# Squared-ReLU MLP in a diffusion backbone: seven products on sums of weight and token parts for 20 of 32 column tiles

## The chip, the cores and the metric

One Trainium2 chip, one core. The metric is the device time of one execution in microseconds (us), the median of three runs. The program is written for the engines directly: each engine (TensorE as PE, VectorE as DVE, ScalarE as ACT, GpSimd as POOL, and SP, which issues most DMAs) runs its own list of instructions in order, and the lists meet only at semaphores.

## The reference

Four layers, each a token mixer (Fourier, gated convolution, RWKV-7, latent attention) followed by a dense MLP, on 512 latent and 128 context tokens (640 columns, T) with D = 1024 features. All is float32. Cut to the MLP:

```
h = rmsnorm(x, g4[2]) * (1 + m[4]) + m[3]          # m: six modulation vectors of the layer
o = square(relu(h @ mlp_w1[i])) @ mlp_w2[i]        # (640 x 1024) @ (1024 x 4096), then @ (4096 x 1024)
x = x + m[5] * rmsnorm(o, g4[3])
```

The modulation vectors are `silu(c) @ mod_w[i] + mod_b[i]`, a matrix of 1024 x 6144 per layer.

## The kernel before

Features lie on the 128 partitions, tokens along the free axis. A weight tile ("slab") is 128 output features by all 1024 inputs, 512 KB. To keep float32 precision each operand is split into a high part (rounded to the type `fp32r`, which PE takes) and a low part (the rest). A product is three matmuls for each block of 128 inputs: high by high, high by low, low by high. SP loads a slab into `wr`, ACT copies it rounded into `ws[..., 0, :]` (`high_part`, line 1757), POOL subtracts (`low_part`, line 771), and PE reads both. `wr` and `ws` have two buffers each, so the loop load, copy, subtract, load goes over two tiles.

The tokens are taken whole (a full tile: 8 blocks x 3 products x 2 halves of 320 tokens = 48 matmuls of 128x320) or by halves (a half tile: 24 matmuls). The MLP of a layer is 32 column tiles of W1 and 32 of W2, the latter in four blocks over the hidden features:

- `in_halves`: 8 tiles of W1 and 8 of W2, first all for the first half of the tokens, then all for the second. The first half overlaps the norm of the rest. PE lines 903 (high) and 913 (low).
- 5 blocks of 8 full tiles: W1, W2, W1, W2, W1 (`unit`, PE lines 882 and 887). For W1, ACT makes the relu (line 2432) and the rounded square (2434); DVE makes the exact square (3340) and its low part (3344) in `hidden_unit`. For W2, DVE adds the tile into `acc` (`out_block`).
- `out_halves`: the last 8 tiles of W2 by halves, with the next norm between them.

Beside the full tiles DVE works on the modulation vectors of the next layer: `mods_beside` takes one or two of 48 tiles per full tile (56 in layer 0, where 8 are left over). A tile (`mod_tile`, line 2711) is two multiply-and-accumulate operations of 128x1024 with `silu` held in PSUM (`silu_near`, copied at line 3368). Its 512 KB come through three or four buffers (`mr`, `mx`) by SP. The lists of ACT, DVE and SP are loops (`Fori`) in this part.

The lists are hand-ordered; each engine takes its instructions strictly in the order of the text, a wait included.

## Time and profile before

| | |
|---|---|
| median of 3 runs | 3523.78 us (3521.26 to 3525.21) |
| profiled execution | 3521.14 us, span 3519.1 us |
| PE busy | 3241.9 us, 92% of the span, 29266 matmuls |
| DVE busy | 1811.0 us, 51% |
| POOL busy | 1564.5 us, 44% |
| ACT busy | 1282.7 us, 36% |
| TensorE clock, mean granted | 0.973 |
| DMA | 465.68 MB, mean 132 GB/s |

Read it so: the shares of busy time are means over very different stages. In the rwkv stage PE waits; in the MLPs it hardly does. Matmuls overlap in the records (each is listed with some 309 ns, though they start 147 ns apart), so for their cost the distance from one start to the next counts.

### The profile page before, as it was taken

How to read it: one execution, taken by the hardware profiler on the slowest of the kernel's cores; microseconds unless marked ns; L12 is line 12 of the kernel's file. 1: busy time of each engine (PE TensorE's matmuls, PEld its weight loads, DVE VectorE, ACT ScalarE, POOL GpSimd, SP SyncE). 2: the span in 40 equal slices, each digit the busy share in tenths (PEclk: the TensorE clock that was granted, in tenths of full speed). 3: DMA queues.
4: the chain of work that ended last, by engine and by line, in shares of the span. 5: the costliest groups of instructions: out<-in, count | busy, mean ns of one | idle time of the engine just before them, and what ended most of it. 6: DMA issues, size and time to landing. Idle time of an engine off the chain costs nothing.

```text
span 3519.1 us, 74842 instructions
## 1 busy us (share of the span) xinstructions
PE 3241.9 (92%) x29266; PEld 3007.5 (85%) x29266; DVE 1811.0 (51%) x3092; ACT 1282.7 (36%) x2148; POOL 1564.5 (44%) x1043
## 2 busy tenths in 40 slices
PE   5899999999999998898688889999998989999998
PEld 2789999899899997796577777999997856899997
DVE  8643765564526555859834444447545643521113
ACT  5343223422532224546423334432234333532223
POOL 0455334554553334535577744643344301563334
PEclk9899999999999999999899999999999999999999
DMA  7544554333345443436734433445443301342223
GB/s 285 161 124 148 195 202 141 121 114 100 113 141 196 158 143 109 124 120 221 238 102 119 119 77 120 126 150 197 148 145 97 99 3 37 114 144 73 77 72 122
DMA packets 209306, 465.68 MB, mean 132 GB/s; under 512 B 89056, under 2 KB 98848, under 8 KB 208544
## 3 DMA queue, kind: packets, MB, share of 16 engines
q1 hardware_dynamic: 179904, 442.50, 39.0%
q10 hardware_dynamic: 29152, 19.65, 1.8%
q8 instruction: 182, 2.98, 0.3%
q14 instruction: 68, 0.56, 0.0%
HBM read 419.71 MB, written 41.06 MB: 131 GB/s over the span
## 4 chain that ended last, share of the span: by engine, by line
issue 65%; POOL 17%; POOLq 8%; PE 5%; DVE 3%; DVEq 1%; ACT 0%; DMA 0%; ACTq 0%; SPq 0%
POOL ws L771 17%; POOLq L811 4%; POOLq L808 3%; PE banks L903 1%; PE banks L882 1%; PE banks L913 1%; PE banks L887 1%; POOLq L779 1%; PE banks L1178 0%; DVE bt L2992 0%; POOLq L817 0%; DVEq L2982 0%; DVEq L3022 0%; DVE ar L3011 0%; DVE bt L3014 0%
## 5 line engine op out<-in xcount | busy, mean ns | idle before, releaser
L771 POOL TENSOR_TENSOR ws<-wr,ws 128x1024 fp32r<-128x1024 f32 x509 | 1239.6, 2436 | 1814.5 <-ACT ws L1757 1813.1
L1757 ACT ACTIVATE ws<-wr 128x1024 fp32r<-128x1024 f32 x509 | 537.8, 1057 | 1029.2 <-PE banks L887 442.0
L882 PE MATMUL banks<-hs,ws 128*128 128x320 f32 x3712 | 564.9, 309 | 0.4 <-DVE acc L2833 0.3
L882 PEld LDWEIGHTS banks<-hs,ws 128*128 128x128 f32 x3712 | 549.0, 188 | 1.6 <-DVE hs L2935 0.7
L903 PE MATMUL banks<-hs,ws 128*128 128x320 f32 (+2 forms) x2624 | 446.2, 320 | 43.8 <-DVE hs L2570 14.2
L903 PEld LDWEIGHTS banks<-hs,ws 128*128 128x128 f32 x2624 | 404.4, 194 | 71.5 <-issue 29.8
L903 PE MATMUL banks<-fs,ws 128*128 128x320 f32 x2304 | 374.3, 312 | 12.8 <-DVE fs L3326 6.4
L2711 DVE SCALAR_TENSOR_TENSOR mjunk<-mr,banks 128x1024 f32<-128x1024 f32 x286 | 337.9, 1219 | 72.2 <-DMA mr<-in_m_slabs 49.2
L903 PEld LDWEIGHTS banks<-fs,ws 128*128 128x128 f32 x2304 | 343.9, 188 | 31.5 <-issue 12.5
L882 PE MATMUL banks<-fs,ws 128*128 128x320 f32 x2048 | 310.8, 309 | 0.0
L882 PEld LDWEIGHTS banks<-fs,ws 128*128 128x128 f32 x2048 | 303.0, 188 | 0.0
L887 PE MATMUL banks<-hs,ws 128*128 128x320 f32 x1856 | 291.0, 309 | 0.0
L887 PEld LDWEIGHTS banks<-hs,ws 128*128 128x128 f32 x1856 | 277.0, 188 | 0.0
L913 PE MATMUL banks<-hs,ws 128*128 128x320 f32 (+2 forms) x1312 | 232.5, 319 | 2.5 <-POOL ws L771 2.5
L2432 ACT ACTIVATE relu<-banks 128x640 f32<-128x640 f32 x92 | 64.9, 705 | 427.1 <-PE banks L887 427.1
L913 PEld LDWEIGHTS banks<-hs,ws 128*128 128x128 f32 x1312 | 206.0, 194 | 13.6 <-issue 8.0
L913 PE MATMUL banks<-fs,ws 128*128 128x320 f32 x1152 | 195.7, 311 | 0.0
L913 PEld LDWEIGHTS banks<-fs,ws 128*128 128x128 f32 x1152 | 174.4, 188 | 3.9 <-POOL ws L771 2.2
L810 POOL TENSOR_TENSOR inv_x<-inv_x,inv_t 80x31 f32<-80x31 f32 (+15 forms) x248 | 151.3, 610 | 36.1 <-issue 1.3
L887 PE MATMUL banks<-fs,ws 128*128 128x320 f32 x1024 | 160.6, 309 | 0.0
L806 POOL TENSOR_TENSOR inv_t<-inv_a,inv_x 80x31 f32<-80x31 f32 (+15 forms) x248 | 143.4, 578 | 36.1 <-issue 1.7
L887 PEld LDWEIGHTS banks<-fs,ws 128*128 128x128 f32 x1024 | 152.8, 188 | 0.0
(332 smaller groups left out, 3960.1 us busy)
## 6 DMA issues: line engine op xcount, KB each, us to landing
wr<-in_w_slabs SPq DMA_DIRECT2D x509, 512.0 KB, 3.6
mr<-in_m_slabs SPq DMA_DIRECT2D x167, 512.0 KB, 5.1
ar_d<-ar SPq DMA_DIRECT2D x16, 640.0 KB, 4.3
bk_d<-bt SPq DMA_DIRECT2D x16, 640.0 KB, 6.1
bk<-bk_d SPq DMA_DIRECT2D x16, 640.0 KB, 5.5
ar<-ar_d SPq DMA_DIRECT2D x32, 320.0 KB, 5.4
mx<-in_m_slabs SPq DMA_DIRECT2D x16, 512.0 KB, 6.6
rkv_d<-relu ACTq DMA_DIRECT2D x16, 320.0 KB, 3.7
```

Of the source, the lines that this page charges most:

```text
L771: pool.tensor_tensor(ws[s % 2][:, 1, :], wr[:, s % 2, :], ws[s % 2][:, 0, :].bitcast(F32), ALU.subtract).then_inc(lo_ready, 1)
L806: pool.tensor_tensor(tj, blocks_in[:, j + 1:32, j:j + 1].to_broadcast(shape), x[:, j:j + 1, 0:j + 1].to_broadcast(shape), ALU.mult)
L808: pool.drain()
L810: pool.tensor_tensor(rows, rows, tj, ALU.add)
L811: pool.drain()
L882: pe.matmul(pu[:, t % 2, h, 0:HT], ws[s % 2][:, 0, k * P:(k + 1) * P], src[:, k, part, h * HT:(h + 1) * HT], start=(k + part == 0), stop=F ...
L887: mm = pe.matmul(pu[:, t % 2, h, 0:HT], ws[s % 2][:, 1, k * P:(k + 1) * P], src[:, k, 0, h * HT:(h + 1) * HT], start=False, stop=(k == KD ...
L903: pe.matmul(pu[:, t % 2, h, 0:q - p], ws[s % 2][:, 0, k * P:(k + 1) * P], src[:, k, c, p:q], start=(k + c == 0), stop=False)
L913: mm = pe.matmul(pu[:, t % 2, h, 0:q - p], ws[s % 2][:, 1, k * P:(k + 1) * P], src[:, k, 0, p:q], start=False, stop=(k == KD - 1))
L1757: act.activation(ws[s % 2][:, 0, :], wr[:, s % 2, :], ACT.Copy).then_inc(hi_ready, 1)
L2432: act.activation(halves(relu[:, j, :]), pu[:, t % 2, :, 0:HT], ACT.Relu).then_inc(relu_ready, 1)
L2711: op = dve.scalar_tensor_tensor(mjunk[:, g, :], at, 0.5, vector[:, g, :], ALU.mult, ALU.mult, accum_out=modt[:, col, g:g + 1].rearrange("p ...
```

## The change

W1's tiles 12 to 31 of each layer are taken in ten pairs. A pair is seen as a matrix of 2 x 2: two column tiles by two halves of the 1024 inputs (A11 to A22, each 128 x 512). The tokens are seen as 2 x 2 too: two halves of the inputs by two halves of the tokens (B11 to B22). The eight products of the plain rule become seven, on four sums of weight parts and four sums of token parts (`t1`, `t2`, `t34`), and the results are added up from PSUM. A product is 4 blocks x 3 = 12 matmuls of 128x320.

- POOL (`weight_pairs`) makes the weight sums in float32: four additions of 128x512 per pair, then one low part per product. ACT makes the high parts and copies three partial results out of PSUM per pair. The operands of PE are in a ring of four places of 128x512 (`wq`, over the old `ws`), so a place is written again only after its last product.
- The token sums are made during the second half of `in_halves`: `combine_copy`, `combine_high` on ACT and `combine_part` on DVE, for four rows in four steps each. `t34` has no room of its own and lies over `x`, so ACT's queue stores `x` (2.6 MB) to `x_d` when the second half starts and reads it back after the last pair; the next use of `x` waits for it.
- W2's tiles 8 to 23 are cut into quarters of 128x512 (`U_ENTRY`), each for four hidden blocks. The first eight pairs have four quarters each: eight products more, whose results DVE adds into `acc` (`take_u`). So a pair has 15 products, the last two pairs have 7.
- Before the pairs stand 4 full tiles of W1 (`regular`).
- The raw pair comes as one load of 1 MB into `wp`, a single new buffer, for the last pair into `wr`. The silu vectors are read back from memory in each of the first three layers (1 MB, through `wp`) in place of lying in SBUF.
- Modulation tiles: two after each of the four full tiles, then five per pair (six in layer 0); `mx` is gone, three buffers are left.
- All lists of this part are written out, no loops.

The core of the diff. PE's order for one pair, where `product(n, step, e, bank, tokens, fresh)` is one product with entry e of the ring:

```diff
+                for n in range(PAIRS):
+                    dense = n >= PAIRS_U
...
+                    if n == 0:
+                        pe.wait_ge(tile_read, t_out - 1)
+                    elif n <= PAIRS_U:
+                        pe.wait_ge(u_taken, u0 - 3)
+                    else:
+                        pe.wait_ge(f_ready, f1 - 2)
+                    product(n, 1, 0, xb, b11, True)
...
+                    product(n, 2, 1, yb_, first, True)
+                    pe.wait_ge(part_copied, copied + 1)
+                    product(n, 3, 2, xb, second, False)
...
+                    product(n, 4, 3, zb, b21, True)
+                    pe.wait_ge(part_copied, copied + 3)
+                    product(n, 5, 4, xb, third, False)
...
+                    product(n, 6, 5, wb, h0, True)
+                    pe.wait_ge(sum_made, summed + 1)
+                    product(n, 7, 6, yb_, b22, False)
+                    product(n, 8, 7, xb, fourth, False)
+                    pe.wait_ge(u_taken, u0 + 1)
+                    product(n, 9, 5, wb, h1, True)
+                    pe.wait_ge(f_ready, f1 + 2)
+                    product(n, 10, 8, zb, h0, True)
+                    pe.wait_ge(f_ready, f1 + 3)
+                    product(n, 11, 8, yb_, h1, True)
+                    pe.wait_ge(f_ready, f1 + 4)
+                    product(n, 12, 9, xb, h0, True)
+                    pe.wait_ge(u_taken, u0 + 2)
+                    product(n, 13, 9, wb, h1, True)
+                    pe.wait_ge(u_taken, u0 + 3)
+                    product(n, 14, 10, zb, h0, True)
+                    pe.wait_ge(u_taken, u0 + 6)
+                    product(n, 15, 10, wb, h1, True)
```

In `product`, PE waits for `e_high` before the 8 matmuls on the high part and for `e_low` before the 4 on the low part. DVE's list:

```diff
+                for i in range(KH):
+                    regular(i)
+                    mods(2)
+                for n in range(PAIRS_U):
+                    mods(2)
+                    dve.drain()
+                    corner_sum(n)
+                    first_sum(n)
+                    dve.drain()
+                    square(n, 0)
+                    square(n, 1)
+                    dve.drain()
+                    square_low(n, 0)
+                    square_low(n, 1)
+                    take_u(n, 0)
+                    second_sum(n)
...
+                    square(n, 2)
+                    square(n, 3)
...
+                    square_low(n, 2)
+                    square_low(n, 3)
+                    take_u(n, 1)
+                    mods(1)
+                    take_u(n, 2)
+                    take_u(n, 3)
+                    mods(1)
+                    take_u(n, 4)
+                    take_u(n, 5)
+                    mods(1)
+                    take_u(n, 6)
+                    take_u(n, 7)
+                    mods(mods_in_pair(l) - 5)
```

`corner_sum` waits for product 5 and adds bank xb and `c_sum`, which lies in SBUF; `square(n, 0)` and `square_low(n, 0)` read only SBUF. POOL's list, and SP's loads of the raw pairs:

```diff
+                sums(0)
+                more_sums(0)
+                for e in range(3):
+                    low(0, e)
+                last_sum(0)
+                low(0, 3)
+                for n in range(PAIRS):
+                    if n < PAIRS_U:
+                        for e in range(4, 11):
+                            low(n, e)
+                        sums(n + 1)
+                        more_sums(n + 1)
+                    elif n < PAIRS - 1:
+                        low(n, 4)
+                        sums(n + 1)
+                        low(n, 5)
+                        low(n, 6)
+                        pool.drain()
+                        more_sums(n + 1)
...
+                    for e in range(3):
+                        low(n + 1, e)
+                    last_sum(n + 1)
+                    low(n + 1, 3)
...
+                def load_pair(m):
+
+                    if m == 0:
+                        sp.wait_ge(t_made, 9 * li + 9)
+                    if m:
+                        sp.wait_ge(e_low, from_ahead + ENTRIES * li + entry_at(m - 1, 10 if m == PAIRS - 2 else 7) + 1
+                                   if m < PAIRS - 1 else from_ahead + ENTRIES * li + entry_at(PAIRS_U - 1, 10) + 1)
+                    to = wr if m == PAIRS - 1 else wp
+                    sp.dma_start(to[:, :, :], a["w_slabs"][d + 2 * m:d + 2 * m + 2].rearrange("s p n -> p s n")
+                                 ).then_inc(p_landed[m == PAIRS - 1], 16)
...
+                load_pair(PAIRS - 1)
+                sp.wait_ge(e_low, from_ahead + ENTRIES * (li + 1))
```

ACT's list for the last two pairs ends, and for the last pair holds the copy of the first slab behind them (`high_part`):

```diff
+                    squared(n, 0)
+                    squared(n, 1)
+                    if n < PAIRS - 1:
+                        highs(n + 1, 1)
+                    else:
+                        act.wait_ge(product_done, product_at(li, n, 5))
+                        high_part(slab[0], None)
+                    positive(n, 2)
+                    act.drain()
+                    squared(n, 2)
...
+                    positive(n, 3)
+                    act.drain()
+                    squared(n, 3)
...
+                act.dma_start(x[:, :, :].rearrange("p k n -> p (k n)"), x_d).then_inc(x_moved, 16)
```

## Rows read from the trace of the kernel before

**Rows 1.** The page's first part, PE: busy time, share of the span, instructions.
```profile
PE 3241.9 (92%) x29266; PEld 3007.5 (85%) x29266; DVE 1811.0 (51%) x3092; ACT 1282.7 (36%) x2148; POOL 1564.5 (44%) x1043
```

**Rows 2.** Windows: stretch, length, busy time of each engine, granted clock, DMA share, GB/s.
```profile
305.00:587.00 282.00, 282.00 (x1925) 282.00 (x1924) 186.16 (x289) 73.23 (x86) 97.74 (x41) 1.00 0.51 179
136.00:140.00 4.00, 4.00 (x24) 3.62 (x17) 0.05 (x1) 1.51 (x4) 2.39 (x1) 0.65 0.51 141
15.00:25.00 10.00, 0.00 (x0) 0.00 (x0) 7.78 (x13) 3.83 (x6) 0.00 (x0) 1.00 1.03 404
```

**Rows 3.** Timeline of PE, full and half tiles: start, length, line, operation, count.
```profile
305.37 4.86 PE L882 MATMUL banks<-hs,ws 128*128 128x320 f32 x32
312.41 4.86 PE L882 MATMUL banks<-hs,ws 128*128 128x320 f32 x32
...
268.92 2.51 PE L903 MATMUL banks<-hs,ws 128*128 128x320 f32 x16
272.44 2.51 PE L903 MATMUL banks<-hs,ws 128*128 128x320 f32 x16
```

**Rows 4.** Groups by line, PE: count, busy, mean ns, idle before, releaser.
```profile
L882 PE MATMUL banks<-hs,ws 128*128 128x320 f32 x3712 | 564.9, 309 | 0.4 <-DVE acc L2833 0.3
```

**Rows 5.** Groups by line and form, DVE.
```profile
L2711 DVE SCALAR_TENSOR_TENSOR mjunk<-mr,banks 128x1024 f32<-128x1024 f32 x286 | 337.9, 1219 | 72.2 <-DMA mr<-in_m_slabs 49.2 <-issue 22.1
...
L2627 DVE TENSOR_TENSOR acc<-banks,acc 128x320 f32<-128x320 f32 x64 | 31.4, 490 | 129.5 <-PE banks L913 119.5 <-PE banks L972 6.1 <-PE banks L948 3.6
```

**Rows 6.** Timeline of DVE, two modulation tiles back to back, their first halves.
```profile
582.70 1.22 DVE L2711 SCALAR_TENSOR_TENSOR mjunk<-mr,banks 128x1024 f32<-128x1024 f32 x1
...
585.16 1.22 DVE L2711 SCALAR_TENSOR_TENSOR mjunk<-mr,banks 128x1024 f32<-128x1024 f32 x1
```

**Rows 7.** Groups by line and form, ACT.
```profile
L1757 ACT ACTIVATE ws<-wr 128x1024 fp32r<-128x1024 f32 x509 | 537.8, 1057 | 1029.2 <-PE banks L887 442.0 <-DMA wr<-in_w_slabs 362.7 <-PE banks L913 180.1
...
L2289 ACT ACTIVATE tr<-banks 128x512 f32<-128x512 f32 x80 | 44.6, 602 | 61.5 <-PE banks L1417 61.5
...
L2006 ACT ACTIVATE reluh<-banks 128x320 f32<-128x320 f32 x64 | 26.8, 418 | 0.0
```

**Rows 8.** Groups by line and form, POOL.
```profile
L771 POOL TENSOR_TENSOR ws<-wr,ws 128x1024 fp32r<-128x1024 f32 x509 | 1239.6, 2436 | 1814.5 <-ACT ws L1757 1813.1 <-issue 0.2
...
L806 POOL TENSOR_TENSOR inv_t<-inv_a,inv_x 80x255 f32<-80x255 f32 x16 | 11.0, 690 | 2.3
```

**Rows 9.** DMA issues: transfer, queue, count, KB each, median us to landing.
```profile
wr<-in_w_slabs SPq DMA_DIRECT2D x509, 512.0 KB, 3.6
...
silu<-silu_d SPq DMA_DIRECT2D x1, 1024.0 KB, 6.8
```

**Rows 10.** Instructions of DVE's line 2524, both inputs in SBUF: shortest, median, longest ns.
```profile
L2524 DVE TENSOR_TENSOR rstd<-root,ident x30: 491/493/1830, 146.5 to 3505.1; 128x320 f32<-128x320 f32 x30
```

**Rows 11.** Timeline of DVE at the first full tile of W1.
```profile
313.46 0.83 DVE L3340 SCALAR_TENSOR_TENSOR ta<-banks,relu 128x640 f32<-128x640 f32 x1 [5.01 <-ACT relu L2432]
...
315.76 1.22 DVE L2711 SCALAR_TENSOR_TENSOR mjunk<-mr,banks 128x1024 f32<-128x1024 f32 x1 [0.31 <-DMA mr<-in_m_slabs]
```

**Rows 12.** Timeline of PE behind two waits (in brackets: idle time and its releaser).
```profile
135.70 0.74 PE L932 MATMUL banks<-sqa,ones 128*32 128x320 f32 x8 [2.53 <-DVE mjunk L2711]
136.38 4.00 PE L903 MATMUL banks<-hs,ws 128*128 128x320 f32 x16
...
622.49 0.35 PE L940 MATMUL banks<-rstd,ones 128*32 128x80 f32 x8 [1.73 <-ACT rstd L1795]
```

**Rows 13.** Timeline of ACT and PE where the second half of the tokens begins.
```profile
251.42 1.06 ACT L1757 ACTIVATE ws<-wr 128x1024 fp32r<-128x1024 f32 x1 [2.40 <-DMA wr<-in_w_slabs]
...
254.04 2.58 PE L903 MATMUL banks<-hs,ws 128*128 128x320 f32 x16 [1.05 <-DVE fs L3326]
```

**Rows 14.** Timeline of ACT and PE in the last block of W2.
```profile
596.21 1.06 ACT L1757 ACTIVATE ws<-wr 128x1024 fp32r<-128x1024 f32 x1 [4.03 <-DMA wr<-in_w_slabs]
...
597.53 2.51 PE L903 MATMUL banks<-fs,ws 128*128 128x320 f32 x16
```

More of the change, by code:

```diff
@@ L450, in build @@
         order = []
+        middles = []
         first_slab = 0
@@ L2052, in in_halves @@
                     take(j, 1)
-                for j in range(mid - 1):
-                    ahead()
+                    if hidden:
+                        combine_part(j, li)
+                for j in range(mid):
+                    if j < mid - 1:
+                        ahead()
+                    combine_part(n + j, li)
                 x_tiles[0] += 2 * KD
@@ new lines, in mlp @@
+            def mlp(li):
+                in_halves(FB, 4, True, li)
+                for i in range(KH):
+                    t = tile[0]
+                    if i < KH - 1:
+                        ahead()
+                    else:
+                        slab[0] += 1
+                        tile[0] += 1
+                        for e in range(2):
+                            entry_high(li, 0, e)
+                    act.wait_ge(tile_done, t + 1)
+                    act.wait_ge(tile_read, t - 1)
+                    act.activation(halves(relu[:, i % 2, :]), pu[:, t % 2, :, 0:HT], ACT.Relu).then_inc(relu_ready, 1)
+                    act.drain()
+                    act.activation(fs[:, i, 0, :], relu[:, i % 2, :], ACT.Square).then_inc(fhalf_ready, 1)
+                weight_pairs(li)
@@ L3401, in mlp @@
-                tile[0] += 5 * FB
-                hidden[0] += 3 * FB + 1
-                relus[0] += 3 * FB + 1
+                    dve.wait_ge(c_landed, xc_in + 16 * (l + 1))
+                    dve.tensor_copy(silu_near[:, :, :], wp[:, :, :])
+                dve.drain()
+                dve.sem_inc(t_made, 1)
+                t_out, mod_next = tile[0] + KH, [-M_LEFT if l == 0 else 0]
+                assert t_out == middle_tile[l]
+                for i in range(KH):
+                    regular(i)
+                    mods(2)
```

610 lines of the change are left out of this document (441 added, 169 removed).

## Prediction

> **What bounds the kernel now.** I read the page first: TensorE (PE) is busy for 92% of the span and no other engine for more than 51% [rows 1]. That share is a mean over stages, so I asked the stage windows for the part that the change replaces, the 40 full tiles of an MLP (W1 tiles and W2 tiles of 640 tokens). There PE is busy 282.00 of 282.00 us at full granted clock [rows 2]. In the timeline one full tile follows the next after 7.04 us, and one half tile (320 tokens) the next after 3.52 us [rows 3]. A full tile is 48 matmuls, so one matmul of 128x320 costs 146.7 ns. The groups say that this holds everywhere: 3712 matmuls of line 882 have 0.4 us of idle time before them [rows 4]. So here a matmul less is worth its full 146.7 ns, and every wait that the new order brings to PE costs its full length. Nothing hides either.
>
> **The saving.** Two column tiles cost 96 matmuls now. As seven products of 12 matmuls they cost 84. Ten pairs in each of four layers: 12 x 10 x 4 = 480 matmuls fewer, 480 x 0.1467 = **70.4 us**. W2's tiles keep their count: eight products per pair are two tiles' worth. A product is 12 x 0.1467 = 1.76 us, a pair with W2 quarters (15 products) 26.4 us, one without (the last two) 12.3 us. The rest is a ledger of waits.
>
> **Prices.** DVE: 0.49 us for an operation of 128x320 with one input in PSUM, 1.22 us for each half of a modulation tile [rows 5]; two such tiles back to back start 2.46 us apart [rows 6]. ACT: 1.06 us for a copy of 128x1024, 0.60 for 128x512, 0.42 for 128x320 [rows 7]. POOL: 2.44 us for 128x1024; no group has 128x512, so from 80x255 at 0.69 us the line between the two gives 1.27 us (half of the large one, 1.22, is the lower bound) [rows 8]. A load of 512 KB lands after 3.6 us; the fastest stretch moved 404 GB/s, so 0.5 MB more ahead of it costs 1.3 us; 1 MB lands between 4.9 us by that sum and the 6.8 us of the one row that has it [rows 2, 9].
>
> **Steady pairs, by laying the four lists side by side** (us from the start of a pair). POOL: 15 operations x 1.27 = 19 of 26.4. ACT: 11 copies, 3 part copies, 8 for relu and square, 12 us. DVE: 19 operations x 0.49, five or six modulation tiles x 2.46 and drains, 22 to 25 us. So none is the bound by its sum; the order decides. Product 5 ends at 8.8; corner sum 9.5; ACT relus 10.2; squares and low parts of the first two quarters to 13.1; the first W2 take 13.6 (product 9 needs it at 14.1). The second sum, two squares and lows end at 17.2, the take behind them 17.7; modulation tile 20.2, two takes 21.3, tile 23.8, takes four and five 24.9. Product 15 needs that fifth take at 24.6. So PE waits about **0.35 us a pair** where there are modulation tiles (layers 0 to 2), none in layer 3. Seven pairs (the first is counted below): 2.5 us a layer. This includes 0.8 us for one DVE square whose inputs both lie in SBUF while POOL works: the trace has 30 operations of such a kind (128x320) with a median of 493 ns and a longest of 1830 [rows 10]. Without it the take is at 24.1, in time, and the term is 0; with the longest at both such operations of a pair it is up to 8.
>
> The Trainium skill, "SBUF — State Buffer", section "SBUF: two separate sides", says that a VectorE operation with two SBUF inputs and a GpSimd operation that reads SBUF exclude each other for a whole instruction. The trace agrees as far as [rows 10] go; by that rule the sum has the 2.5 us, without it 0.
>
> **First pair, layers 0 to 2.** Before, one or two modulation tiles went beside each full tile; now two follow each of four W1 tiles and two more stand before the first corner sum. From the trace, DVE takes its first tile 8.1 us after PE began it [rows 11, 3], a W1 tile's two operations cost 2.1 (2.30 to the tile behind them, less the most of its 0.31 wait for a load). From 8.1: 4 x 2.1 + 10 x 2.46 = 33.0, so 41.1, and the corner sum ends at 41.6. PE wants it before product 7, at 4 x 7.04 + 6 x 1.76 = 38.7. Wait 2.9 us. After a wait of 2.53 us the trace shows 16 matmuls in 4.00 us, where others take 2.51, with the granted clock at 0.65 of full, between its levels 2.4 and 1.2 GHz; after 1.73 us the matmuls kept their pace [rows 2, 3, 12]. So add 1.5: **4.5 us** a layer (2.9 to 7), x 3 = 13.5. Queued behind those tiles on SP is the slab of the fourth W1 tile: its load waits for a modulation buffer, about 15.4, and it comes just in time; no extra.
>
> **Second half of the first 16 tiles.** Sixteen combination steps go onto ACT and DVE, and x (2.6 MB) is stored from ACT's queue just as this half starts. Sums fit: ACT gets 4 x 0.42 more in every other tile of 3.5 us. But ACT takes a tile's relu only after its next slab copy, which waits for the slab's DMA, and PE waits for that take already (1.05 us) [rows 13]. So a load made 1.3 us longer by the store goes to PE in full; DVE's four extra operations (2 us) before a take add some 1.2 over the half. **2.5 us** x 4 = 10; nothing as lower bound, 6 with two loads hit and the clock lowered. The load of 1 MB for the modulation vectors now stands among these slabs (layers 0 to 2): 2.6 us of transfer, less about 2 of slack: 0.7 x 3 = 2.
>
> **Into the last two pairs.** SP loads pair 8 only after POOL's last low part of pair 7, at 19.5 on pair 7's time. Landed at 24.5 to 26.3, then three sums and a low part, 5.1: 29.6 to 31.4. PE needs it at 26.4 + 1.2. From there POOL has 15 operations (19.0 us) up to the first low part of pair 9, while PE's matmuls up to it last 13.5. Pair 9 can so end at 24.5 + 19.0 + 0.6 + 6 x 1.76 = 54.7 (26.3: 56.5) where the products alone end at 51.0. **4.5 us** x 4 = 18, bounds 3 (POOL at 1.22) and 6.5.
>
> **Into the second matrix's last tiles.** Now the loads run ahead and PE goes on at once; ACT's copy ends just before its tile, 596.21 + 1.06 against 597.53 [rows 14]. After the change the raw pair 9 lies in both slab buffers, so the first slab can be loaded only after POOL's very last low part, 2.0 before pair 9 ends. 3.6 for the load and 1.06 for the copy: PE idle 2.7. ACT does its last two squares only after that copy, and PE waits for them after 14 matmuls: 0.5. x is read back (6.5 us of transfer) beside the next slab: 1.3 more, partly under a lowered clock (up to 1.5). **4.5 us** x 4 = 18, bounds 2.5 and 9. x itself is wanted 28 us later: hidden.
>
> **Sum.** Waits 7.5 + 13.5 + 10 + 2 + 18 + 18 = 69. Against the saving: -1.4. The profiled execution took 3521.1 us for a span of 3519.1; the median of the three runs is 3523.8, 2.7 above it. 3521.1 - 1.4 + 2.7 = **3522 us**. All lower bounds: 0 + 8.7 + 0 + 0 + 12 + 10 = 31, 3484. All upper ones: 24 + 21 + 24 + 6 + 26 + 36 = 137, 3590.
>
> **Rivals.** (1) The same waits, near their lower bounds, because one wait gives the other engines the time that the next would have cost: total about 35, so 3488. For it: the terms are laid out one after the other, and PE's wait into pair 8 lets DMA and ACT run ahead. Against: the two waits for loads have fixed lengths that no engine shortens. (2) Slower: the fifth take decides. If both operations on the corner sum wait for POOL, or a modulation tile waits for its load, it comes 1.5 us late in every pair; 8 x 3 x 1.5 = 36 in place of 7.5: 3550. It decides from 24.6 us on; my own time for it is 24.9, so the margin is thin. (3) The change doesn't bring its saving: PE waits on two semaphores per 12 matmuls in place of two per 24 or 48. If each product lost 0.1 us, 536 products would give 54: 3576. Against: half tiles with as many matmuls per wait as now 24 and 8 run at 146.7 ns [rows 3].
>
> **Chances.** The ledger as summed, 3507 to 3540: 0.46. Rival 1: 0.33. Rival 2: 0.17. Rival 3: 0.04. A measurement tells 0.2% (7 us) from no change. Faster: rival 1 and a fifth of the first, 0.42; same: half of the first, 0.23; slower: the rest, 0.35. The range 3488 to 3556 leaves out the ends of both sides; as both signs hold much chance, the likeliest case's own is 3507 to 3540.
>
> **What would show it.** Right: products 1.76 us apart; PE idle near 3 us before product 7 of the first pair with DVE as releaser, 2 to 4 us in product 1 of pair 8 behind POOL, about 3 us before the first tile of the last W2 block behind ACT and a slab load. Wrong: a wait in every pair much over 0.35 us (rival 2), these three below 1 us each (rival 1), or a product longer than 1.76 us without a wait (rival 3).

## Result and the profile after

The changed kernel takes 3555.9 us (median of 4 runs, 3554.1 to 3566.8), the kernel before 3523.5 beside it: ratio 1.0099, 95% interval 1.0078 to 1.0120: 32 us slower by the medians, 35 by the ratio, which the table of experiments uses. Forecast were 3522 us, 3507 to 3540 for the likeliest case, and most of the chance on faster or the same; the result lies above that, at the end of the wider range (3556). The profiled execution took 3556.7 us for a span of 3554.9, 35.8 more than before.

The page of the changed kernel: the first part, then groups by line (the answers to [rows 1, 4, 8]) and DMA issues (to [rows 9]).

```profile
PE 3209.8 (90%) x28786; PEld 2971.0 (84%) x28786; DVE 2062.0 (58%) x3756; ACT 1481.6 (42%) x2812; POOL 1944.1 (55%) x1467
...
L1059 PE MATMUL banks<-hs,ws 128*128 128x320 f32 (+2 forms) x2624 | 452.7, 324 | 62.3 <-DVE fs L3729 24.6
...
L1059 PE MATMUL banks<-fs,ws 128*128 128x320 f32 x2304 | 386.6, 319 | 43.9 <-ACT ws L2014 28.1
...
L1897 PE MATMUL banks<-fs,wq 128*128 128x320 f32 x2048 | 342.0, 309 | 0.0
...
L903 POOL TENSOR_TENSOR wq<-wp,wq 128x512 fp32r<-128x512 f32 x144 | 185.3, 1298 | 16.7 <-issue 11.3
...
L1897 PE MATMUL banks<-hs,wq 128*128 128x320 f32 x960 | 163.1, 313 | 11.6 <-DVE c_sum L3776 9.7
...
wr<-in_w_slabs SPq DMA_DIRECT2D x429, 512.0 KB, 3.7
...
wp<-in_w_slabs SPq DMA_DIRECT2D x36, 1024.0 KB, 5.1
x_d<-x ACTq DMA_DIRECT2D x4, 2560.0 KB, 9.0
x<-x_d ACTq DMA_DIRECT2D x4, 2560.0 KB, 10.0
```

The reader is to see three things. PE has 480 matmuls less, and is busy only 32.1 us less. The products (L1897) have hardly an idle moment: 0.0 in the largest group, 11.6 us in the one whose waits are those of the first pairs. Most of the new idle time sits in L1059, the half tiles on either side of the new part: 62.3 and 43.9 us, where the same two groups of the kernel before (L903) had 43.8 and 12.8. And x's transfers last 9 and 10 us.

To place it, I took from PE's timeline the start of each stage in each layer, and the distances between them (us; layers 0, 1, 2, 3). "Last block" runs to the next stage's first matmul, in layer 3 to the end of the span. The forecast's ledger stands beside them as the sum over four layers.

| stage | before | after | more, 4 layers | forecast |
|---|---|---|---|---|
| second half of the first 16 tiles | 59.8 60.9 59.8 59.9 | 66.1 67.8 68.4 67.0 | +29.0 | +12 |
| 4 full tiles of W1 (28.2) | | 29.3 29.5 28.4 28.2 | +2.8 | 0 |
| first pair (26.4) | | 34.3 30.8 30.8 26.7 | +17.0 | +13.5 |
| pairs 1 to 7 (184.8) | | 184.8 in each | -0.1 | +7.5 |
| last two pairs (24.6) | | 30.5 30.3 30.1 30.4 | +22.8 | +18 |
| gap ahead of the last block | | 2.8 2.9 3.0 3.0 | +11.8 | with the last block |
| last block of W2 | 67.7 76.3 65.4 79.2 | 72.6 83.6 72.4 85.5 | +25.5 | +18 with the gap |
| all waits | | | +108.8 | +69 |
| matmuls saved | | | -70.4 | -70.4 |
| the rest of the kernel | | | -2.4 | 0 |

In brackets stand the lengths at 146.7 ns a matmul. Sum +36.0, the spans say +35.8.

Now the two large rows. Timeline of the changed kernel, ACT and PE, where the second half begins in layer 0 (answers to [rows 13]):

```profile
247.79 0.33 ACTq L2333 DMA_DIRECT2D x_d<-x  x1
...
252.22 1.06 ACT L2014 ACTIVATE ws<-wr 128x1024 fp32r<-128x1024 f32 x1 [3.37 <-DMA wr<-in_w_slabs]
...
254.85 3.43 PE L1059 MATMUL banks<-hs,ws 128*128 128x320 f32 x16 [2.02 <-DVE fs L3729]
...
259.56 1.06 ACT L2014 ACTIVATE ws<-wr 128x1024 fp32r<-128x1024 f32 x1 [4.00 <-DMA wr<-in_w_slabs]
...
262.19 3.86 PE L1059 MATMUL banks<-hs,ws 128*128 128x320 f32 x16 [2.06 <-DVE fs L3729]
```

Read it from below: PE waits for `fs`, the low part of DVE's square, which waits for ACT's relu, which stands behind a slab copy, which waited 4.00 us for its DMA. Before, PE waited 1.05 us at the first place [rows 13] and 0.17 at the second. And after each wait 16 matmuls take 3.4 to 3.9 us in place of 2.6.

The last block in layer 0 (answers to [rows 14]), and under it the DMA queues in the 10 us from x's read-back on; q10 is ACT's queue, q1 is SP's (packets, MB, share of the 16 engines' time; then issue, KB each, median us to landing):

```profile
592.06 1.06 ACT L2014 ACTIVATE ws<-wr 128x1024 fp32r<-128x1024 f32 x1 [2.75 <-DMA wr<-in_w_slabs]
...
593.17 3.81 PE L1059 MATMUL banks<-fs,ws 128*128 128x320 f32 x16 [2.66 <-ACT ws L2014]
...
594.42 0.33 ACTq L2845 DMA_DIRECT2D x<-x_d  x1
...
595.77 3.10 SPq L530 DMA_DIRECT2D wr<-in_w_slabs  x2
...
605.10 1.06 ACT L2014 ACTIVATE ws<-wr 128x1024 fp32r<-128x1024 f32 x1 [9.18 <-DMA wr<-in_w_slabs]
...
606.20 4.63 PE L1059 MATMUL banks<-fs,ws 128*128 128x320 f32 x16 [4.20 <-ACT ws L2014]
```

```profile
q10 hardware_dynamic: 144, 2.62, 68.5%
q1 hardware_dynamic: 221, 0.85, 20.6%
...
x<-x_d ACTq DMA_DIRECT2D x1, 2560.0 KB, 10.2
wr<-in_w_slabs SPq DMA_DIRECT2D x2, 512.0 KB, 8.5
```

The first slab was issued at 595.8, 1.3 us behind x's transfer, and was there at 605.1, 9.3 us later and 0.5 us after x had landed; the second took 7.7 us (8.5 is the median of the two). A slab takes 3.7 us elsewhere. PE stood 4.20 us for it.

The trace has each packet's start, and the delay has two parts. Packets first: x goes in 144 for 2.62 MB, a slab in 144 for 0.52 MB; 16 of each are 4 bytes long, the other 128 are 20,480 bytes (x) and 4,096 bytes (slab). The queues in the first 3.4 us after the slab was issued (595.8 to 599.2), and in the 5.3 us after that (599.2 to 604.5):

```profile
q10 hardware_dynamic: 53, 1.09, 79.9%
```

```profile
q10 hardware_dynamic: 79, 1.29, 56.7%
q1 hardware_dynamic: 230, 0.88, 40.5%
```

In the first window SP's queue has no packet at all: the slab's first one comes 3.45 us after its issue, where a slab that meets no x transfer has it after 0.96 us (median of 217 in this kernel). In the second window the slab shares the engines with packets five times as long, and needs 5.9 us from its first packet to landing, where it needs 2.7 alone.

Windows of the two stages, the kernel before and then the changed one (stretch, length, busy time and instructions of each engine, granted clock, DMA share, GB/s):

```profile
245.00:305.00 60.00, 57.71 (x388) 56.55 (x387) 11.87 (x24) 23.54 (x33) 39.88 (x17) 1.00 0.48 148
...
587.00:655.00 68.00, 63.48 (x448) 58.51 (x448) 25.44 (x54) 31.18 (x52) 38.51 (x16) 1.00 0.42 125
```

```profile
245.00:311.00 66.00, 60.52 (x385) 59.32 (x384) 32.15 (x68) 34.05 (x64) 39.29 (x17) 0.95 0.54 188
...
593.00:666.00 73.00, 67.39 (x446) 62.31 (x447) 24.41 (x52) 31.10 (x53) 40.68 (x17) 0.93 0.45 153
```

In the second half PE is idle 5.5 us (66.00 less 60.52) where it was 2.3, and busy 2.8 us longer for the same matmuls, at a granted clock of 0.95 in place of 1.00: after the waits it ran for a time at 1.2 GHz, not 2.4. In the last block it is idle 1.1 us more and busy 3.9 us more. So in the second half the clock costs about as much as the added waits, in the last block more.

The first pair of layer 0, DVE and PE:

```profile
348.56 1.30 DVE L3144 TENSOR_TENSOR modt<-modt,modb 128x16 f32<-128x16 f32 x1
349.93 1.19 DVE L3150 SCALAR_TENSOR_TENSOR coef<-modt,ng 128x16 f32<-128x16 f32 x1
...
356.24 0.49 DVE L3776 TENSOR_TENSOR c_sum<-banks,c_sum 128x320 f32<-128x320 f32 x1 [0.16 <-issue]
...
356.78 2.50 PE L1897 MATMUL banks<-hs,wq 128*128 128x320 f32 x8 [5.04 <-DVE c_sum L3776]
```

PE waits for the corner sum as forecast, but 5.0 us in place of 2.9: the modulation coefficients (L3144, L3150; 348.56 to 351.24, 2.7 us) fall between the tiles in this layer.

A steady pair, pair 2 of layer 0, which starts at 401.50 (DVE):

```profile
411.58 1.33 DVE L3803 SCALAR_TENSOR_TENSOR c_sum<-c_sum,reluh 128x320 f32<-128x320 f32 x1 [0.19 <-ACT reluh L2787]
...
413.40 0.49 DVE L3812 SCALAR_TENSOR_TENSOR fs<-c_sum,fs 128x320 fp32r<-128x320 f32 x1
413.81 0.48 DVE L3815 TENSOR_TENSOR fs<-banks,fs 128x320 fp32r<-128x320 f32 x1
...
423.98 1.09 DVE L3825 TENSOR_TENSOR acc<-banks,acc 128x320 f32<-128x320 f32 x2
```

The square with both inputs in SBUF takes 1.33 us, as the ledger's 0.8 us more had it: of the kernel's 40 such squares 31 begin while POOL works, and 30 of these take 1.33 to 1.59 us; the other ten take 0.49. Even so takes four and five (the last line) are done at 425.07, 23.6 us after the pair's start, where 24.9 was forecast and product 15 wants them at 24.6. For DVE operations listed with 0.49 us follow one another after 0.4 us (413.40 to 413.81), and the forecast had priced them at 0.49.

### The profile page after: what moved, and what is told of

Read it like the earlier page. It is cut to its first block, busy times and chain, and to the rows that moved or that the text cites. A ratio compares the mean times of both kernels' runs of the same rounds, so it can differ in the third digit from the quotient of the medians.

```text
span 3554.9 us, 73409 instructions
## 1 busy us (share of the span) xinstructions
PE 3209.8 (90%) x28786; PEld 2971.0 (84%) x28786; DVE 2062.0 (58%) x3756; ACT 1481.6 (42%) x2812; POOL 1944.1 (55%) x1467
## 4 chain that ended last, share of the span: by engine, by line
issue 38%; PE 32%; POOL 12%; POOLq 10%; DVE 4%; DMA 1%; DVEq 1%; ACT 1%; ACTq 0%; SPq 0%
PE banks L1897 15%; POOL ws L844 10%; PE banks L1901 7%; POOLq L959 3%; PE banks L1059 3%; POOLq L956 3%; PE banks L1038 3%; PE banks L1069 2%; POOL wq L903 2%; PE banks L1043 1%; POOLq L870 1%; DMA wr<-in_w_slabs 1%; DVE mjunk L3127 1%; DVE mr L3127 1%; PE banks L1334 0%
## 5 line engine op out<-in xcount | busy, mean ns | idle before, releaser
L844 POOL TENSOR_TENSOR ws<-wr,ws 128x1024 fp32r<-128x1024 f32 x365 | 892.1, 2445 | 1199.9 <-ACT ws L2014 1199.3
L1059 PE MATMUL banks<-hs,ws 128*128 128x320 f32 (+2 forms) x2624 | 452.7, 324 | 62.3 <-DVE fs L3729 24.6
L1059 PEld LDWEIGHTS banks<-hs,ws 128*128 128x128 f32 x2624 | 411.0, 197 | 90.5 <-issue 49.3
L1059 PE MATMUL banks<-fs,ws 128*128 128x320 f32 x2304 | 386.6, 319 | 43.9 <-ACT ws L2014 28.1
L1059 PEld LDWEIGHTS banks<-fs,ws 128*128 128x128 f32 x2304 | 354.4, 193 | 64.8 <-ACT ws L2014 37.5
L1897 PE MATMUL banks<-fs,wq 128*128 128x320 f32 x2048 | 342.0, 309 | 0.0
L1897 PEld LDWEIGHTS banks<-fs,wq 128*128 128x128 f32 x2048 | 310.9, 188 | 0.1
L903 POOL TENSOR_TENSOR wq<-wr,wq 128x512 fp32r<-128x512 f32 x144 | 185.8, 1301 | 207.7 <-ACT wq L2762 206.4
L1897 PE MATMUL banks<-t,wq 128*128 128x320 f32 x1280 | 218.4, 314 | 0.0
L1069 PEld LDWEIGHTS banks<-hs,ws 128*128 128x128 f32 x1312 | 206.5, 195 | 11.6 <-issue 6.0
L1897 PEld LDWEIGHTS banks<-t,wq 128*128 128x128 f32 x1280 | 199.5, 193 | 0.0
L1069 PE MATMUL banks<-fs,ws 128*128 128x320 f32 x1152 | 196.8, 312 | 0.0
L903 POOL TENSOR_TENSOR wq<-wp,wq 128x512 fp32r<-128x512 f32 x144 | 185.3, 1298 | 16.7 <-issue 11.3
L3127 DVE SCALAR_TENSOR_TENSOR mr<-mr,banks 128x1024 f32<-128x1024 f32 x159 | 193.4, 1217 | 0.0
L1901 PE MATMUL banks<-fs,wq 128*128 128x320 f32 x1024 | 191.7, 309 | 0.0
L1069 PEld LDWEIGHTS banks<-fs,ws 128*128 128x128 f32 x1152 | 176.8, 190 | 3.4 <-POOL ws L844 2.1
L1038 PE MATMUL banks<-hs,ws 128*128 128x320 f32 x1152 | 176.7, 310 | 2.8 <-ACT ws L2014 2.0
L1038 PEld LDWEIGHTS banks<-hs,ws 128*128 128x128 f32 x1152 | 170.2, 188 | 4.7 <-issue 2.8
L1897 PE MATMUL banks<-hs,wq 128*128 128x320 f32 x960 | 163.1, 313 | 11.6 <-DVE c_sum L3776 9.7
```

The costliest lines, as they stand in the source:

```text
L844: pool.tensor_tensor(ws[s % 2][:, 1, :], wr[:, s % 2, :], ws[s % 2][:, 0, :].bitcast(F32), ALU.subtract).then_inc(lo_ready, 1)
L903: pool.tensor_tensor(slot[:, 1, :], from_w, slot[:, 0, :].bitcast(F32), ALU.subtract).then_inc(e_low, 1)
L1038: pe.matmul(pu[:, t % 2, h, 0:HT], ws[s % 2][:, 0, k * P:(k + 1) * P], src[:, k, part, h * HT:(h + 1) * HT], start=(k + part == 0), stop=F ...
L1059: pe.matmul(pu[:, t % 2, h, 0:q - p], ws[s % 2][:, 0, k * P:(k + 1) * P], src[:, k, c, p:q], start=(k + c == 0), stop=False)
L1069: mm = pe.matmul(pu[:, t % 2, h, 0:q - p], ws[s % 2][:, 1, k * P:(k + 1) * P], src[:, k, 0, p:q], start=False, stop=(k == KD - 1))
L1897: pe.matmul(out, wq[:, slot, 0, k * P:(k + 1) * P], src(k, c), start=(fresh and k + c == 0), stop=False, skip_group_check=True)
```

## The experiments

Theory A: slabs that are issued beside x's store or read-back land only when that ends, and this is where the forecast went wrong. Theory B: the cause is the work that the change puts on ACT, DVE and POOL (combination steps, sums), and x's bytes are cheap. Ratios are to the kernel before on the same chip; "us" is the ratio's distance from 1 times 3523. The first four ran together, and so did each three or two after them.

| kernel | median us | ratio (95%) | us to before |
|---|---|---|---|
| changed | 3555.9 | 1.0099 (1.0078 to 1.0120) | +35 |
| x moved as 32 KB | 3514.9 | 0.9976 (0.9960 to 0.9991) | -8 |
| pair 8 read earlier | 3548.7 | 1.0066 (1.0040 to 1.0092) | +23 |
| modulation tiles later | 3550.2 | 1.0075 (1.0057 to 1.0094) | +26 |
| pair 9 in other buffers | 3551.0 | 1.0081 (1.0055 to 1.0107) | +29 |
| x in 8 transfers | 3521.4 | 1.0006 (0.9995 to 1.0018) | +2 |
| all four repairs | 3488.6 | 0.9912 (0.9896 to 0.9929) | -31 |
| kernel before, x stored twice a layer | 3556.9 | 1.0102 (1.0085 to 1.0119) | +36 |
| x in 2 transfers | 3543.7 | 1.0065 (1.0048 to 1.0083) | +23 |
| x in 4 transfers | 3530.1 | 1.0023 (1.0013 to 1.0034) | +8 |
| x in 1 transfer, short rows | 3543.1 | 1.0062 (1.0044 to 1.0079) | +22 |
| x in 8 transfers, long rows | 3558.6 | 1.0104 (1.0084 to 1.0123) | +37 |
| all four, x in 1 with short rows | 3509.3 | 0.9972 (0.9959 to 0.9986) | -10 |

**x moved as 32 KB.** x is not saved, so `t34` can't lie over it: the third and fourth token sums are written over the first two, and the products that need them read those. So this kernel leaves out the traffic and the right tokens of two sums; every step is still made.

```diff
-act.dma_start(x_d, x[:, :, :].rearrange("p k n -> p (k n)"))
+act.dma_start(x_d[:, 0:64], x[:, 0, 0:64])
...
-act.dma_start(x[:, :, :].rearrange("p k n -> p (k n)"), x_d)
+act.dma_start(x[:, 0, 0:64], x_d[:, 0:64])
...
-return t34[:, k, c, :]
+return t1[:, k, c, :]
```

> The changed kernel with the store of x and its read-back cut from 2.6 MB to 32 KB each; x isn't overwritten, because the third and fourth token sums go over the first and second (all combination steps are still made, with one drain more in each group of four; the products on these sums use other data). So what is left out is the traffic, the correct tokens of two sums per pair, and nothing else that takes time. Theory A (the two x transfers hold back the weight slabs that are loaded beside them, and PE waits): the second half of the first 16 tiles (67 us in the changed kernel, 60 before) loses 5 to 6 us per layer, the last W2 block 5 to 7 per layer; in all 40 to 50 us, so 0.994 to 0.998 of the time before. Theory B (the combination steps on ACT and DVE and the late first slab make these waits, the traffic only adds 1.3 us as predicted): at most 12 us less than the changed kernel, ratio 1.006 or above.

The second half is back at 61.1, 61.4, 61.6 and 60.9 us (before 59.8 to 60.9), the last block at 65.7, 77.2 and 65.9 in layers 0 to 2. The stages between keep their waits. Some 43 us of the slowdown hang on x's transfers; all the combination steps, still there, leave 0.5 to 1.9 us a layer in the second half, 4.7 in all. So x's transfers are the cause in these two stages, as theory A had it, and B falls there; whether a slab has to wait for the transfer's end is a question for the later runs.

**Pair 8 read earlier**, one line, in the entry of the ring for which SP waits:

```diff
-entry_at(m - 1, 10 if m == PAIRS - 2 else 7)
+entry_at(m - 1, 7)
```

> One wait changed: the raw weights of pair 8 are loaded once POOL has made the low part of entry 7 of pair 7 (the last that reads the raw buffer), as for all earlier pairs, not entry 10. Theory A (the late load starts POOL's chain late; dense pairs now last 30.5 us for 24.6 of products): the 2.3 us wait and the slow clock behind it go, POOL's own pace leaves 1.5 to 2 us: 3.5 to 4 us per layer, 14 to 16 in all, ratio about 1.0055. Theory B (POOL's 22 operations of 1.3 us up to the last low part, against 24.6 us of products, are the bound, whenever they start): under 1.5 us per layer, ratio 1.009.

The last two pairs take 28.0, 28.9, 27.5 and 27.8 us in place of 30.1 to 30.5, for 24.6 of matmuls. So the late load was 2.3 us a layer, less than theory A's 3.5 to 4. The wait that is left is POOL's: 2.9 to 4.3 us a layer. The changed kernel (three sums, then the low part that PE wants):

```profile
557.87 1.30 POOL L869 TENSOR_TENSOR ws_sum<-wp 128x512 f32<-128x512 f32 x1 [5.02 <-DMA wp<-in_w_slabs]
...
562.22 1.26 POOL L903 TENSOR_TENSOR wq<-wp,wq 128x512 fp32r<-128x512 f32 x1 [0.16 <-issue]
```

```profile
563.54 1.43 PE L1901 MATMUL banks<-hs,wq 128*128 128x320 f32 x4 [2.32 <-POOL wq L903]
```

and with pair 8 read earlier, where the wait has moved to pair 9:

```profile
574.98 0.85 PE L1901 MATMUL banks<-hs,wq 128*128 128x320 f32 x4 [2.09 <-POOL wq L903]
```

**Modulation tiles later**: the two behind the last W1 tile and the two ahead of the first corner sum go one each into pairs 0 to 3.

```diff
-mods(mods_in_pair(l) - 5)
+mods(tail(l, n))      # (1 if l == 0 else 0) + (1 if n < 4 else 0)
...
-    mods(2)
+    mods(lead(n))      # 2 if n else 0
```

> Four modulation tiles are moved: none after the fourth W1 tile and none ahead of the first corner sum; one more in each of the first four pairs (five to six, in layer 0 six to seven, four in the first pair where it had five, in layer 0 five where it had six). SP's loads follow. Theory A (these four stand ahead of the corner sum that PE waits for, 5 us and 2.5 us of slow clock in layer 0): 5 to 8 us less in each of layers 0 to 2, 15 to 22 in all, ratio 1.004 to 1.0055. Theory B (DVE has no room for them later; the fifth W2 take then misses product 15 in four pairs): what the first pair gains comes back as waits of 1 to 2.5 us in the four pairs, ratio 1.008 to 1.010.

The first pair takes 27.0, 26.7, 26.7 and 26.7 us: its waits are gone in all layers. But pairs 1 to 7 of layer 0 take 188.6 in place of 184.8, so that the ratio comes out between the two theories. Windows of layer 0, pairs 1 to 7, the changed kernel and then this one:

```profile
375.00:559.00 184.00, 184.00 (x1256) 184.00 (x1256) 163.31 (x300) 75.48 (x152) 129.17 (x101) 1.00 0.59 196
```

```profile
362.00:550.00 188.00, 185.16 (x1256) 183.84 (x1255) 170.23 (x320) 76.51 (x152) 131.85 (x104) 1.00 0.60 201
```

Three of its pairs have seven modulation tiles, and each costs PE 1.3 us; six in a pair (layer 0 as changed, layers 1 and 2 here) cost nothing. This is the margin of which rival 2 spoke, measured: it lies between six and seven tiles, not at five.

**Pair 9 in other buffers**: its raw weights go into two modulation buffers, so the last block's slabs no longer wait for them.

```diff
-w = wr if n == PAIRS - 1 else wp
+w = mr if n == PAIRS - 1 else wp
...
 load_pair(PAIRS - 1)
-sp.wait_ge(e_low, from_ahead + ENTRIES * (li + 1))
+load_until(p_mid + 2)
```

> The raw weights of the last pair are loaded into the buffers of the modulation tiles, which are free by then, not into the two slab buffers, so the first two slabs of the last W2 block can be loaded during the last pairs. Theory A (the first slab is late because pair 9 lies in its buffer): the 2.7 us of PE idle time in front of the block and the slow clock behind it go, and with slabs one and two early the third comes earlier too: 4 to 6 us per layer, 16 to 24 in all, ratio 1.003 to 1.005. Theory B (the wait in this block is set by the read-back of x): the third slab still lands only after x, PE waits there longer by what it gained, and the total falls by less than 8 us, ratio 1.0075 or above.

The gap falls from 2.9 to 0.06 us in every layer, and the last block stays at 72.5, 83.9 and 72.0. Its wait is another one, as theory B had it:

```profile
602.18 4.39 PE L1062 MATMUL banks<-fs,ws 128*128 128x320 f32 x16 [5.04 <-ACT ws L2017]
```

**x in 8 transfers** of 320 KB, one beside each tile:

```diff
 for j in range(mid):
     ahead()
     round_two()
+    act.dma_start(x_d[:, k * T:(k + 1) * T], x[:, k, :])    # k = 0, 4, 1, 5, ...
 for m in range(KD):
     ahead()
+    act.dma_start(x[:, m, :], x_d[:, m * T:(m + 1) * T])
```

> The changed kernel, with the whole computation, but x (2,560 KB) goes out in eight transfers of 320 KB, one beside each column tile at the end of the first half's tiles of W1, and comes back in eight, one beside each column tile of W2's last block. Theory A (the weight slabs issued beside x's one large transfer land only when that ends): each piece is short, so no slab waits 8 us: the second half returns from 66 to 68 us a layer to 61 to 63, the last block with what follows from 72.4 to 67, together 8 to 10 us a layer, 3556 goes to 3515 to 3525. Theory B (the bandwidth that x takes is what costs, however it is cut): the same bytes move beside the same tiles, so within 6 us of 3556. A third outcome, 3530 to 3545, would say that ScalarE's time to issue 16 transfers, or pieces that still collide with the slabs, takes a third to a half of it back.

Second half 62.3, 61.1, 62.3 and 61.5, last block 67.0, 77.6 and 67.7. All the bytes are moved and 33 us are back. The places have changed with the size: the store now runs beside the last eight tiles before the second half, and the read-back is spread over the last block.

**All four repairs.**

> The changed kernel, whole computation, with x in pieces, pair 8 read earlier, the modulation tiles taken out of the first two pairs, and pair 9 in buffers apart from the slabs of W2's last block. If the four waits stand behind one another and apart (each run alone gave 41, 7, 6 and 5 us against the changed kernel), they add: 3556 less 53 to 59, 3497 to 3503, under the kernel before. If they are one queue's delay seen at four places, the sum is less than x alone gives and one other: 3510 to 3520. Between (3503 to 3510) would say that part of each is the slower clock that follows a wait, which a later wait brings back.

The four add up: alone they give 12, 9, 6 and 33 us, together 66, against 60 by addition, which the intervals of some 7 us each don't tell apart; 3488.6 lies below the 3497 to 3503 that was expected. This version is 0.9% faster than the kernel before. Its pairs' stages are 48 us shorter than before's full tiles, of 70.4 saved; what is missing is the last two pairs (27.4 to 29.4 us a layer for 24.6), the seven-tile pairs of layer 0 (3.8), 2.5 in the full tiles and 1.5 in the first pairs. The second half still has 8 us over four layers more than before.

**The kernel before, x stored twice a layer.** No product is changed; two transfers of x stand where the changed kernel stores and reads back.

```diff
+act.dma_start(x_d, x[:, :, :].rearrange("p k n -> p (k n)"))   # where the second half starts
...
+act.dma_start(x_d, x[:, :, :].rearrange("p k n -> p (k n)"))   # ahead of W2's last block
```

> The kernel before, with its own products, and two transfers of x's 2,560 KB to DRAM in each layer, at the places where the changed kernel stores x and reads it back (both are stores here, so that x is left alone). Theory A (one large transfer on another queue holds the slabs back until it ends): the second half goes from 59.8 to 64 to 66 us a layer, the last block with what follows from 67 to 70 to 72, so 3523 goes to 3545 to 3570 with no product changed. Theory C (the delay needs the changed kernel's own schedule: its slabs are issued when GpSimd has made a low part, so they are late to begin with): the kernel before has its slabs issued far enough ahead, 3523 to 3530.

As theory A has it. Second half 66.9, 67.1, 66.8 and 66.9 us, 6.2 to 7.1 more than without the store. Last block 69.3, 79.8, 68.5, only 1.5 to 3.5 more, since here its first slabs had been loaded ahead. Timeline and DMA queues (248 to 259 us) of this kernel:

```profile
248.22 0.33 ACTq L2055 DMA_DIRECT2D x_d<-x  x1
...
259.82 1.06 ACT L1760 ACTIVATE ws<-wr 128x1024 fp32r<-128x1024 f32 x1 [5.49 <-DMA wr<-in_w_slabs]
```

```profile
262.44 4.61 PE L906 MATMUL banks<-hs,ws 128*128 128x320 f32 x16 [3.66 <-DVE fs L3337]
```

```profile
q10 hardware_dynamic: 144, 2.62, 55.5%
q1 hardware_dynamic: 277, 1.04, 32.5%
```

**x in two and in four.**

```diff
+act.dma_start(x_d[:, k * T:(k + 4) * T], ...)    # at every fourth tile; in the other kernel (k + 2), every second
```

> The changed kernel, whole computation, x out in two transfers of 1,280 KB, four tiles apart, and back in two, four tiles apart. In one transfer x takes 9 to 10 us to land and costs 41 us against 32 KB; in eight, each under 4 us, it costs about 6. Theory A (a slab issued beside a transfer lands when that ends, so the price is what the transfer lasts beyond the slab's own slack): 1,280 KB would take some 5 to 6 us to land, the slab behind it loses at most 2 to 3 us against 3.6 us alone, of which the 0.5 to 1 us of slack is taken, and each of the 16 transfers then costs 0.5 to 1.5 us: 3525 to 3540, nearer to the eight pieces than to the one. Theory B2 (the price goes by the bytes, and the eight pieces got it back by being spread over the tiles): about half way, 3535 to 3545.

> The same with four transfers of 640 KB each way, two tiles apart. Theory A: 640 KB lands in about 4 us, no later than a slab of 512 KB does, so nothing is left to lose against eight pieces: 3518 to 3527. Theory B2: a quarter of the way from eight pieces to one, 3525 to 3532.

One, two, four and eight transfers cost +35, +23, +8 and +2. It goes down step by step; both results lie above what theory A gave for them and inside what B2 gave. But this series changes more than the size: with the transfer, the contiguous row in DRAM gets shorter too (20,480 bytes a partition, 10,240, 5,120, 2,560), and from one to more the places change. The next two go at row length and size.

**One transfer with short rows, eight with long ones.**

```diff
-x_d = nc.dram_tensor("x_d", [P, KD * T], F32).ap()
+x_d = nc.dram_tensor("x_d", [KD, P, T], F32).ap().rearrange("k p n -> p k n")
```

```diff
-act.dma_start(x_d[:, k * T:(k + 1) * T], x[:, k, :])
+act.dma_start(x_d[r, :], x[r, :, :].rearrange("p k n -> p (k n)"))    # r = slice(16 * j, 16 * j + 16)
```

> The changed kernel, whole computation, x still in one transfer of 2,560 KB each way, but laid out in DRAM by column tile, so that its pieces of contiguous memory are 2,560 bytes in place of 20,480. In the changed kernel's trace x's transfer is 144 packets for 2.62 MB and a slab is 144 packets for 0.52 MB; in the window of the collision both queues' packets pass one for one. Theory P (the queues take turns packet by packet, so x's long packets give it five times the slab's bytes): with packets shorter than the slab's 4 KB the slab gets more than half, and the single transfer costs no more than the eight pieces did: 3515 to 3528. Theory A (a slab lands when the transfer that it meets has ended, whatever its packets): nothing changes but perhaps a longer transfer: 3550 to 3562.

> The changed kernel, whole computation, x in eight transfers of 320 KB each way, at the places of the earlier run with eight, but each takes 16 partitions with their whole 20,480 bytes in place of 128 partitions with 2,560. Theory P: a slab meets at most one or two long packets per engine, so each piece still delays it by the time of its own bytes (about 1 us), more than the short ones: 3524 to 3535. Theory A: as the eight short pieces, 3516 to 3526. If eight long pieces cost as much as the one transfer (over 3545), it is the packet's length alone, whatever the size.

Neither theory has either result: 3558.6 lies above both of their ranges, 3543.1 between them. Eight transfers with long rows, which theory A gave +0, cost as much as one: +37, 35 more than eight short ones of the same 320 KB at the same places. That isn't row length alone, though. Rows of 20,480 bytes leave only 16 partitions for a transfer, and ACT's queue takes 58.6% of 25 us (225 to 250) for 1.97 MB, 7.4 us of all 16 engines a MB, where the one large transfer, with the same rows on 128 partitions, takes 2.6 (68.5% of 10 us for 2.62 MB):

```profile
q10 hardware_dynamic: 192, 1.97, 58.6%
```

How the 35 us divide between the longer rows and the fewer partitions, no run shows. The clean run on row length is the single transfer: with short rows in place of long ones it goes from +35 to +22, which theory P gave nothing. ACT's copies between the eight long transfers wait for slabs again and again:

```profile
238.93 1.06 ACT L2014 ACTIVATE ws<-wr 128x1024 fp32r<-128x1024 f32 x1 [4.79 <-DMA wr<-in_w_slabs]
...
247.90 1.06 ACT L2014 ACTIVATE ws<-wr 128x1024 fp32r<-128x1024 f32 x1 [5.35 <-DMA wr<-in_w_slabs]
...
256.67 1.06 ACT L2014 ACTIVATE ws<-wr 128x1024 fp32r<-128x1024 f32 x1 [5.48 <-DMA wr<-in_w_slabs]
```

In the one with short rows (245 to 262 us) x's 2.62 MB go in 1040 packets, SP's are served between them, and the transfer lasts 11.3 us:

```profile
q10 hardware_dynamic: 1040, 2.62, 43.5%
q1 hardware_dynamic: 551, 2.05, 31.3%
```

```profile
250.16 1.06 ACT L2014 ACTIVATE ws<-wr 128x1024 fp32r<-128x1024 f32 x1 [4.46 <-DMA wr<-in_w_slabs]
```

The Trainium skill, "DMA: Bandwidth & Descriptors", section "Queues, rings and completion order", says that each DMA engine takes turns between the queues at the granularity of a packet. The packet counts agree with it: while both queues are served in the changed kernel, about as many packets of SP's pass as of ACT's, 20 and 16 in the microsecond from 600 us on. The +22 of the single transfer with short rows is not explained by it, for short packets don't bring the slab's first packet forward. Queues of this kernel in the last block, 590.5 to 594.1 us, just after a slab was issued at 590.46:

```profile
q10 hardware_dynamic: 460, 1.18, 93.1%
```

Again SP's queue has no packet; the first comes after 3.7 us. This slab lands 6.9 us after its issue, and 3.6 us before x does, so theory A's rule is gone too. The same reading of the packets' starts, for the slabs that were issued while one of x's transfers was in flight and SP's queue was otherwise empty (medians in us, ranges in brackets):

| x's transfers (kernels) | slabs | issue to first packet | first packet to landing |
|---|---|---|---|
| none in flight (changed) | 217 | 0.96 | 2.7 |
| 2,560 KB, rows of 20,480 bytes (changed) | 7 | 3.9 (3.4 to 5.0) | 5.3 |
| the same, kernel before with stores | 7 | 3.8 (3.3 to 4.8) | 3.3 |
| 2,560 KB, rows of 2,560 (both such kernels) | 12 | 4.0 (2.9 to 4.9) | 3.2 |
| 1,280 KB, rows of 10,240 | 16 | 3.6 (1.9 to 4.1) | 2.3 |
| 640 KB, rows of 5,120 | 16 | 1.8 (1.0 to 2.4) | 2.8 |
| 320 KB, rows of 2,560 | 4 | 1.4 (1.1 to 1.5) | 2.5 |
| 320 KB, rows of 20,480 on 16 partitions | 23 | 1.3 (1.0 to 2.7) | 3.6 |

So the time before the first packet goes with the size of the transfer in flight, whatever its rows. The time behind it is longest where long rows are still in flight; in the kernel before with stores four of the seven slabs were issued only 4.2 us behind x, and met less of it. Each of the two theories had one part. What holds the first packet back no run shows.

**All four, x in one with short rows.**

> All four repairs as in the earlier run (3488.6 us), but x in one transfer each way with short contiguous pieces in place of eight transfers. Theory P: the same time within 5 us, 3484 to 3494, and with less for ScalarE to issue. Theory A: the slab waits of x come back, 3520 to 3530.

21 us slower than with eight short transfers (0.9972 against 0.9912), the same distance as without the other repairs (1.0062 against 1.0006, 20 us), and between the two theories once more. So short rows and a small transfer are both needed, as the table above has it.

## Why the prediction was wrong

- **The saving.** Right. 29266 less 28786 are 480 matmuls; pairs 1 to 7 take 184.8 us in every layer, 26.4 each, as forecast.
- **Prices.** Right: 128x512 on POOL 1.30 us (1.27 from the line through its neighbours), 1 MB in 5.1 us (4.9 to 6.8).
- **Steady pairs.** 7.5 us given, none found, in any layer. The slow square was there in most pairs (1.33 us), but DVE's fifth take was in time with five and with six tiles: the list had charged 0.49 us for operations that follow after 0.4. Rival 2, though its 3550 lies near the result, is wrong; and so is rival 3, since the 105 products of pairs 1 to 7 take 1.76 us each.
- **First pair.** Mechanism right, 17.0 us for 13.5. Layers 1 and 2 had 4.4 each for 4.5; layer 0 had 7.9, as the coefficients' step (2.7 us) stood in no list of mine. Layer 3 had 0.3.
- **Full tiles.** The slab of the fourth W1 tile was to come "just in time; no extra". In layer 0 PE waited 0.90 us for its copy; the four layers cost 2.8 us.
- **Into the last two pairs.** Mechanism right, 5.7 us a layer for 4.5, inside the bounds (3 to 6.5).
- **Second half of the first 16 tiles, and the last block: the step that failed.** "So a load made 1.3 us longer by the store goes to PE in full", and for the read-back "1.3 more". The price was taken from bandwidth: 0.5 MB more at 404 GB/s, as if only as many bytes of x as the slab has could get ahead of it. But the slab's first packet came 2.5 to 4 us late, and then it shared the engines with packets five times as long. In layer 0 it landed after 8.0 us in the second half and 9.3 in the last block, in place of 3.6: 4.4 and 5.7 us longer, not 1.3, and in the second half PE waited 2 us at two tiles in a row. With the clock after each wait, x's two transfers cost 43 us (+35 less -8, the run with 32 KB), for which the ledger had 8 x 1.3 = 10.4. That is 33 of the 34 us between forecast and result; the other errors (+3.5 first pair, +5 last two pairs, +3 full tiles, -7.5 steady pairs, -2.5 elsewhere) cancel to 1 or 2. The gap of 2.7 us ahead of the block, which was in the ledger, came as forecast (2.9).
- **The clock.** It was charged once behind each long wait (1.5 us). In the two stages of layer 0 it cost 2.8 and 3.9 us, beside 3.2 and 1.1 us of idle time more.
- **Rival 1** (one wait gives the others time, 35 us in all) is refuted: the waits come to 108.8 us, and the repairs add up.

Left open: what the second half's last 1.2 to 2 us a layer (on average, with x as 32 KB and with all four repairs) are. The combination steps are the candidate by exclusion; no run took them out alone. Open too are what delays a slab's first packet while a large transfer is in flight, and how much of the eight long transfers' 35 us their 16 partitions make.

## What to carry to other kernels

Don't price a large transfer beside a stream of just-in-time loads by its bytes: ask how large it is, how many loads it meets, and how long its packets are against theirs. If it must be moved, cut it both ways, into transfers no larger than a load and with contiguous rows no longer than the load's, one beside each step; here this took the same bytes from 43 us to 10. Price an engine's operations by the distance from one start to the next, not by the listed length. And when a change takes matmuls out of a bound engine but puts waits in, count with each wait the time at the lower clock behind it.

## What was unexpected in the hardware

- A slab issued while a transfer of 2,560 KB is in flight on the other queue has its first packet 2.9 to 5.0 us after its issue, with x in packets of 20,480 or of 2,560 bytes alike; alone it has it after 0.96.
- Eight transfers of 320 KB, with contiguous rows of 2,560 bytes on 128 partitions or of 20,480 bytes on 16, cost 2 and 37 us. The long ones land after 4.6 and 5.3 us, the short ones after 4.0 and 3.2; the harm is to the other queue's loads.
- One store of 2,560 KB beside slabs whose copies wait for their loads already makes that stage 6.2 to 7.1 us longer in each of four layers, where its bytes at 404 GB/s [rows 2] are 6.5 us of transfer.
- Two DVE operations of 128x16, both inputs in SBUF, took 1.30 and 1.19 us while POOL worked; the second one's form takes 0.18 elsewhere (median of 15). The squares of 128x320 with both inputs in SBUF took 1.33 us or more in 30 of the 31 cases that began while POOL worked, 0.49 in the nine others.
